# One low-part operation per dense value block, written over its raw block, with four raw buffers and products of 512, 512 and 384 columns

## The chip, the cores and the metric

The kernel runs on one core of a Trainium2 chip. A core has five engines with an instruction stream each: TensorE (PE; its weight loads are listed apart as PEld), VectorE (DVE), ScalarE (ACT), GpSimd (POOL) and SyncE (SP), which here issues the plain DMAs. They meet only at semaphores. Sixteen DMA engines move data between the chip's memory (HBM) and the on-chip buffer of 128 partitions (SBUF). Products are accumulated in PSUM. The metric is the time of one execution on the device in microseconds (us); lower is better.

## The reference

One layer of a hybrid encoder over 256 tokens of width 2048: an RMS norm, one combined projection, forgetting attention and a gated recurrence, their merge with an output projection, and then a PEER layer, a second residual and a final RMS norm. The change touches the last part of the PEER layer alone:

```python
def peer_layer(x, wq, keys, U, Vt):
    ...
    # for each token: 8 heads x 16 experts, idx (T, 8, 16) out of 16384, gate = softmax of their scores
    def blk(args):
        xb, ib, gb = args
        u = U[ib]
        hid = jax.nn.gelu(jnp.einsum('td,thkd->thk', xb, u))
        v = Vt[ib]
        return jnp.einsum('thk,thkd->td', gb * hid, v)
```

Each token thus adds 128 rows of the value table `Vt` (16384 x 2048), each with its own weight `gb * hid`.

## The kernel before

All work is float32. Where TensorE multiplies, an operand is split into a high part, its rounding to the type `fp32r`, and a low part, the rest; a product is the sum of high x high, high x low and low x high.

The value sum is done in two ways at once. Of each row of `Vt` the last 640 columns (`CW`) are fetched only for the experts that were chosen: GpSimd issues 256 indirect DMAs (2 token tiles x 128 choices), each of 128 rows of 640 columns, 328 KB, into a ring of five buffers `starts`, and VectorE multiplies each with its token's weight and adds it to `X` (line 1411; `add_start(s)`). The first 1408 columns (`DW`) are done densely. The 16384 experts are 128 blocks of 128. For each block the whole 128 x 1408 piece of the table (721 KB) is loaded, and multiplied from the left with a 128 x 256 matrix of weights (expert of the block by token, most entries zero), which an earlier stage has scattered into `weight_of`.

For block `n` the engines do this, each in the order of its own loop over the blocks:

- SP loads `v_raw[n % 3]` (line 363). From block 3 on it first waits on `v_ready` until both low parts of block n - 3 are written.
- ScalarE writes the high part `v_hi[n % 2]` (line 771) when the load has landed and block n - 2 is used up. Before every even block it also writes `e_hi`, the high parts of the weights of two blocks (line 762).
- VectorE writes the low part in two pieces, 768 and 640 columns, into a single buffer `v_lo` (line 1420). Each piece waits for `v_used`, until TensorE has used the same piece of the block before. Behind each piece stands one `add_start`. After every second block come two operations for `e_lo` (line 1400).
- TensorE (lines 1770 to 1772) does for each piece and each of the two token tiles (`acc` for the first, `scr` for the second, both in PSUM) three products for each run of columns: 512 and 256 in the first piece, 256 and 384 in the second. It adds one to `v_used` after each piece. That is 24 products a block.

GpSimd issues the gather for `starts[s % 5]` (line 487) when `x_added` says that add s - 5 is done. So the gather for s + 5 starts after add s. An add waits for its gather and for the add before it.

The code is written out in this order, with no scheduler; each engine goes through its own list.

## Time and profile before

| | us |
|---|---|
| three runs | 2193.09, 2183.55, 2193.47; median 2193.09 |
| profiled execution | 2183.11, span 2181.4 |
| PE busy | 1477.1 (68%) |
| DVE busy | 1641.9 (75%) |
| ACT busy | 837.4 (38%) |
| POOL busy | 975.7 (45%) |
| dense loads, 128 of 704 KB, from issue to landing | 6.4 (median) |
| gathers of 640 columns, 256, from issue to landing | 6.6 (median) |

The profile is that of one execution. Its busy shares are means over stages that have different limits: projections up to some 870 us, the gathers and dot products for the hidden values up to about 1600 us, and from 1663 to 2164 us the stage that the change touches. An engine's instruction is followed in the views by what ended the idle time before it. Starts and durations overlap somewhat on VectorE and TensorE, because an instruction begins before the one ahead of it has written all its results; so the distance from start to start is what one costs in a row.

### The profile page before, as it was taken

Reading aid. Unit: us, or ns where it says so; the run is one execution under the profiler, and the core shown is the slowest. Engines: PE = TensorE matmul, PEld = TensorE weight load, DVE = VectorE, ACT = ScalarE, POOL = GpSimd, SP = SyncE. Lnnn points to the kernel's source line nnn. Section 1 sums busy time; section 2 is a strip of 40 time slices with the busy share of each in tenths; the row PEclk is TensorE's granted clock in tenths of the full one; section 3 lists DMA queues with packets and bytes.
Section 4 is the critical chain, followed back from the end, with each engine's and each line's share of the span. In section 5 each row is a group of like instructions: output and inputs, shape, how many; then the busy total and the mean of one; then the engine's idle time right before and its main releaser. Section 6 shows DMA issues by size and latency. Waiting matters only on the chain.

```text
span 2181.4 us, 26401 instructions
## 1 busy us (share of the span) xinstructions
PE 1477.1 (68%) x9809; PEld 1368.3 (63%) x9809; DVE 1641.9 (75%) x2172; ACT 837.4 (38%) x1008; POOL 975.7 (45%) x692
## 2 busy tenths in 40 slices
PE   6999999999999999700000000113358999999996
PEld 6987998899999889700000000113247999899996
DVE  5465774545654555798898899998878999999997
ACT  4353433333433444112121221446666444444443
POOL 1002220000000000188888878877747776667763
PEclk9999999999999999855555555555569999999998
DMA  5555443434455554399999999999905999999996
GB/s 194 173 175 191 137 153 126 155 136 158 171 174 175 194 192 168 144 422 421 418 415 414 416 386 404 419 404 369 359 26 191 357 359 354 346 369 356 360 357 224
DMA packets 151526, 597.80 MB, mean 274 GB/s; under 512 B 14688, under 2 KB 14704, under 8 KB 118000
## 3 DMA queue, kind: packets, MB, share of 16 engines
q0 software_dynamic: 58048, 356.02, 41.3%
q1 hardware_dynamic: 93360, 240.22, 31.2%
q8 instruction: 72, 1.18, 0.2%
q14 instruction: 46, 0.38, 0.0%
HBM read 594.09 MB, written 2.10 MB: 273 GB/s over the span
## 4 chain that ended last, share of the span: by engine, by line
PE 47%; issue 15%; DVE 14%; DMA 11%; POOL 8%; ACT 4%; DVEq 0%; POOLq 0%; SPq 0%; ACTq 0%
PE acc L1470 9%; PE acc L1473 8%; PE acc L1472 8%; DMA slots<-in_peer_u,expert 8%; DVE slots L1331 7%; POOL starts L487 6%; DMA starts<-in_v_gather,expert 3%; PE acc L1487 3%; PE acc L1489 3%; PE acc L1488 3%; PE scr L1740 3%; POOL slots L450 1%; PE scr L1535 1%; PE acc L1770 1%; PE acc L1772 1%
## 5 line engine op out<-in xcount | busy, mean ns | idle before, releaser
L798 DVE TENSOR_TENSOR w_lo<-raw,w_hi 128x2048 fp32r<-128x2048 f32 x136 | 314.7, 2315 | 319.5 <-ACT w_hi L503 318.5
L1331 DVE SCALAR_TENSOR_TENSOR slots<-slots,acc 128x2048 f32<-128x2048 f32 x189 | 428.3, 2284 | 36.4 <-DMA slots<-in_peer_u,expert 34.6
L503 ACT ACTIVATE w_hi<-raw 128x2048 fp32r<-128x2048 f32 x136 | 260.1, 1913 | 435.6 <-PE acc L1473 308.0
L487 POOL DMA_INDIRECT starts<-in_v_gather,expert x256 | 344.5, 1346 | 155.4 <-DVE X L1411 103.8
L450 POOL DMA_INDIRECT slots<-in_peer_u,expert x256 | 250.5, 979 | 288.8 <-DVE expert L1267 188.4
L458 POOL TENSOR_TENSOR slots<-slots,N 128x2048 f32<-128x2048 f32 x63 | 285.6, 4533 | 31.6 <-DMA slots<-in_peer_u,expert 31.2
L1470 PE MATMUL acc<-hT_hi,w_hi 128*128 128x256 f32 x1024 | 294.6, 288 | 3.1 <-PE acc L1473 2.5
L1472 PE MATMUL acc<-hT_lo,w_hi 128*128 128x256 f32 x1024 | 292.2, 285 | 0.0
L1473 PE MATMUL acc<-hT_hi,w_lo 128*128 128x256 f32 x1024 | 292.1, 285 | 0.0
L1740 PE MATMUL scr<-hot_a,hot_b 128*128 128x128 f32 x512 | 101.4, 364 | 280.5 <-ACT hot_a L732 171.9
L771 ACT ACTIVATE v_hi<-v_raw 128x1408 fp32r<-128x1408 f32 x128 | 177.0, 1384 | 282.3 <-PE scr L1772 203.6
L1740 PEld LDWEIGHTS scr<-hot_a,hot_b 128*128 128x128 f32 x512 | 88.8, 263 | 293.3 <-issue 283.1
L698 ACT ACTIVATE slots<-slots 128x2048 f32<-128x2048 f32 x63 | 120.3, 1910 | 393.1 <-POOL slots L458 393.1
L1420 DVE TENSOR_TENSOR v_lo<-v_raw,v_hi 128x768 fp32r<-128x768 f32 (+1 forms) x256 | 227.6, 889 | 31.6 <-PE scr L1772 27.9
L1411 DVE SCALAR_TENSOR_TENSOR X<-starts,weight,X 128x640 f32<-128x640 f32 x256 | 225.1, 879 | 8.5 <-DMA starts<-in_v_gather,expert 8.3
L1470 PEld LDWEIGHTS acc<-hT_hi,w_hi 128*128 128x128 f32 x1024 | 199.1, 194 | 5.7 <-issue 5.7
L1472 PEld LDWEIGHTS acc<-hT_lo,w_hi 128*128 128x128 f32 x1024 | 199.0, 194 | 0.0
L1473 PEld LDWEIGHTS acc<-hT_hi,w_lo 128*128 128x128 f32 x1024 | 198.8, 194 | 0.0
L1770 PE MATMUL acc<-v_hi,e_hi 128*128 128x256 f32 (+2 forms) x512 | 167.7, 328 | 8.2 <-DVE v_lo L1420 8.1
L1772 PE MATMUL acc<-v_hi,e_lo 128*128 128x256 f32 (+2 forms) x512 | 165.9, 324 | 0.0
L1771 PE MATMUL acc<-v_lo,e_hi 128*128 128x256 f32 (+2 forms) x512 | 165.7, 324 | 0.0
L1771 PE MATMUL scr<-v_lo,e_hi 128*128 128x256 f32 (+2 forms) x512 | 165.6, 323 | 0.0
(262 smaller groups left out, 3324.1 us busy)
## 6 DMA issues: line engine op xcount, KB each, us to landing
raw<-in_w_in SPq DMA_DIRECT2D x88, 1024.0 KB, 4.8
v_raw<-in_v_dense SPq DMA_DIRECT2D x128, 704.0 KB, 6.4
raw<-in_w_o SPq DMA_DIRECT2D x16, 1024.0 KB, 5.1
raw<-in_peer_wq SPq DMA_DIRECT2D x16, 1024.0 KB, 5.0
raw<-in_w_a_up SPq DMA_DIRECT2D x8, 1024.0 KB, 5.1
raw<-in_w_b_up SPq DMA_DIRECT2D x8, 1024.0 KB, 5.0
slots<-in_peer_u,expert POOLq DMA_INDIRECT x256, 9.0
starts<-in_v_gather,expert POOLq DMA_INDIRECT x256, 6.6
```

The lines of the kernel that those rows point to most:

```text
L450: pool.indirect_dma_start(slots[:, j, :], None, u_rows, bass.IndirectOffsetOnAxis(ap=expert[:, t, k:k + 1], axis=0)).then_inc(row_landed[j ...
L458: g.tensor_tensor(slots[:, j, :], slots[:, j, :], N1[:, q // NSEL, :], ALU.mult).then_inc(product_ready, 1)
L487: pool.indirect_dma_start(starts[s % CRING][:, :], None, v_gather[:, :], bass.IndirectOffsetOnAxis(ap=expert[:, s // NSEL, s % NSEL:s % NS ...
L503: a.activation(w_hi[:, m % 2, :, :], raw[:, m % 2, :, :], ACT.Copy).then_inc(hi_ready, 1)
L798: v.tensor_tensor(w_lo[:, m % 2, :, :], raw[:, m % 2, :, :], w_hi[:, m % 2, :, :].bitcast(fp32), ALU.subtract).then_inc(lo_ready, 1)
L1331: v.scalar_tensor_tensor(out=slots[:, j, :], in0=slots[:, j, :], scalar=1.0, in1=row, op0=ALU.mult, op1=ALU.mult, accum_out=hid[:, t, k:k + 1]
L1420: v.tensor_tensor(v_lo[:, cols], v_raw[n % RAWS][:, cols], v_hi[:, n % 2, cols].bitcast(fp32), ALU.subtract).then_inc(v_ready, 1)
L1470: t_.matmul(to, wh, hi_[:, kk, :], start=kk == 0 and f % 2 == 0, stop=False, skip_group_check=True)
L1472: t_.matmul(to, wh, lo_[:, kk, :], start=False, stop=False, skip_group_check=True)
L1473: last = t_.matmul(to, wl, hi_[:, kk, :], start=False, stop=last_k, skip_group_check=True)
L1740: last = t_.matmul(scr[:, n % 2, (SC + c) * P:(SC + c + 1) * P], hot_b[:, n % 2, c, :], hot_a1[:, n % 4, c, :] if t else hot_a[:, n % 2, c ...
L1771: t_.matmul(to, eh, v_lo[:, cols], start=False, stop=False, skip_group_check=True)
```

## The change

The low part of a block is written by one VectorE operation of 1408 columns instead of two. It goes into the same memory as the block's raw data: `v_lo[n]` is a view at the address of `v_raw[n]`, of which there are now four (the fourth lies where the single `v_lo` was). The operation no longer waits for `v_used`. Both `add_start` of a block stand behind it, one after the other. TensorE waits for `v_ready` once a block, does its three products for runs of 512, 512 and 384 columns for each token tile, and adds one to `v_used` at the block's end. Since the raw buffer now also holds the low part, SP waits for `v_used` of block n - 4 before it loads block n. ScalarE's and GpSimd's waits on `v_used` are restated in blocks.

```diff
--- before.py
+++ after.py
@@ -49,12 +49,11 @@
 SC = 4
 CW = 640
 DW = D - CW
-VHALF = (slice(0, 768), slice(768, DW))
-VPIECES = (((0, 512), (512, 768)), ((768, 1024), (1024, DW)))
+VPIECES = ((0, 512), (512, 1024), (1024, DW))
 BLOCKS = P
 BATCHES = P // SC
 CRING = 5
-RAWS = 3
+RAWS = 4
 PIECES = 4
 SPREAD_FROM, SPREAD_TWICE = 44, 52
 IJ_GROUP = 56
@@ -206,8 +205,10 @@
         weight_of1 = at("weight_of1", 32, [P, P])
         weight_of = [[at(f"weight_of0_{q}", kib, [P // PIECES, P]) for q, kib in enumerate((16, 128, 144, 168))],
                      [weight_of1[:, q * P // PIECES:(q + 1) * P // PIECES, :] for q in range(PIECES)]]
-        v_raw = [at(f"v_raw{n}", kib, [DW]) for n, kib in enumerate((112, 117.5, 105))]
-        v_hi, v_lo = at("v_hi", 184, [2, DW], f32r), at("v_lo", 160, [DW], f32r)
+        VALUES_AT = (112, 117.5, 105, 160)
+        v_raw = [at(f"v_raw{n}", kib, [DW]) for n, kib in enumerate(VALUES_AT)]
+        v_lo = [at(f"v_lo{n}", kib, [DW], f32r) for n, kib in enumerate(VALUES_AT)]
+        v_hi = at("v_hi", 184, [2, DW], f32r)
         e_hi, e_lo = at("e_hi", 97, [2, NT, 2 * P], f32r), at("e_lo", 101, [2, NT, 2 * P], f32r)
         gain_f = at("gain_f", 16, [D])
         starts = [at(f"starts{n}", kib, [CW]) for n, kib in enumerate((123, 125.5, 195, 197.5, 165.5))]
@@ -368,8 +369,9 @@
             load_v(1)
             sp.wait_ge(scattered, 2 + NT * P // SC)
             load_v(2)
+            load_v(3)
             for n in range(RAWS, BLOCKS):
-                sp.wait_ge(v_ready, 2 * (n - RAWS) + 2)
+                sp.wait_ge(v_used, n - RAWS + 1)
                 sp.sem_inc(granted_w, 1)
                 load_v(n)
             for n in range(2 * NT):
@@ -476,7 +478,7 @@
 
             for s in range(NT * NSEL):
                 if s == NSEL:
-                    pool.wait_ge(v_used, 2 * P // PIECES)
+                    pool.wait_ge(v_used, P // PIECES)
                     pool.dma_start(gain_f[:, :], norm_f_g.rearrange("(l f) -> l f", l=1).partition_broadcast(P)
                                    .rearrange("q l f -> q (l f)")).then_inc(gain_f_in, 16)
                 if s == CRING - 1:
@@ -756,7 +758,7 @@
             def high_e(pair):
 
                 if pair >= 2:
-                    act.wait_ge(v_used, 4 * pair - 4)
+                    act.wait_ge(v_used, 2 * pair - 2)
                 q, at0 = 2 * pair // (P // PIECES), 2 * pair % (P // PIECES)
                 for t in range(NT):
                     last = a.activation(e_hi[:, pair % 2, t, :],
@@ -767,7 +769,7 @@
             for n in range(BLOCKS):
                 act.wait_ge(v_landed[n % RAWS], 16 * (n // RAWS + 1))
                 if n >= 2:
-                    act.wait_ge(v_used, 2 * (n - 2) + 2)
+                    act.wait_ge(v_used, n - 1)
                 a.activation(v_hi[:, n % 2, :], v_raw[n % RAWS][:, :], ACT.Copy).then_inc(v_hi_ready, 1)
                 if n % 2 and n + 1 < BLOCKS:
                     high_e((n + 1) // 2)
@@ -1414,18 +1416,17 @@
             low_e(0)
             for n in range(BLOCKS):
                 dve.wait_ge(v_hi_ready, n + 1)
-                for c, cols in enumerate(VHALF):
-                    if n:
-                        dve.wait_ge(v_used, 2 * (n - 1) + c + 1)
-                    v.tensor_tensor(v_lo[:, cols], v_raw[n % RAWS][:, cols], v_hi[:, n % 2, cols].bitcast(fp32),
-                                    ALU.subtract).then_inc(v_ready, 1)
-                    add_start(2 * n + c)
+                lows = v_lo[n % RAWS][:, :]
+                v.tensor_tensor(lows, v_raw[n % RAWS][:, :], v_hi[:, n % 2, :].bitcast(fp32),
+                                ALU.subtract).then_inc(v_ready, 1)
+                add_start(2 * n)
+                add_start(2 * n + 1)
                 if n % 2 and n + 1 < BLOCKS:
                     low_e((n + 1) // 2)
             dve.wait_ge(x_added, NT * NSEL)
 
             y = [acc[:, :, :].rearrange("p a n -> p (a n)"), scr[:, :, :].rearrange("p a n -> p (a n)")]
-            dve.wait_ge(v_used, 2 * BLOCKS)
+            dve.wait_ge(v_used, BLOCKS)
             for t in range(NT):
                 v.tensor_tensor(X[:, t, CW:D], y[t][:, 0:DW], X[:, t, CW:D], ALU.add).then_inc(y_summed, 1)
             dve.wait_ge(squared, 1 + 4 * NT + NT)
@@ -1759,19 +1760,17 @@
             for n in range(BLOCKS):
                 pe.wait_ge(e_ready, n // 2 + 1)
                 e_cols = slice(n % 2 * P, (n % 2 + 1) * P)
-                for c in range(2):
-                    pe.wait_ge(v_ready, 2 * n + c + 1)
-                    for t in range(NT):
-                        flat = (acc, scr)[t][:, :, :].rearrange("p a n -> p (a n)")
-                        eh, el = e_hi[:, n // 2 % 2, t, e_cols], e_lo[:, n // 2 % 2, t, e_cols]
-                        for at0, end in VPIECES[c]:
-                            to, cols = flat[:, at0:end], slice(at0, end)
-                            clear, stop = n == 0 and at0 % GW == 0, n == BLOCKS - 1
-                            t_.matmul(to, eh, v_hi[:, n % 2, cols], start=clear, stop=False, skip_group_check=True)
-                            t_.matmul(to, eh, v_lo[:, cols], start=False, stop=False, skip_group_check=True)
-                            last = t_.matmul(to, el, v_hi[:, n % 2, cols], start=False, stop=stop,
-                                             skip_group_check=True)
-                    last.then_inc(v_used, 1)
+                pe.wait_ge(v_ready, n + 1)
+                for t in range(NT):
+                    flat = (acc, scr)[t][:, :, :].rearrange("p a n -> p (a n)")
+                    eh, el = e_hi[:, n // 2 % 2, t, e_cols], e_lo[:, n // 2 % 2, t, e_cols]
+                    for at0, end in VPIECES:
+                        to, cols = flat[:, at0:end], slice(at0, end)
+                        clear, stop = n == 0, n == BLOCKS - 1
+                        t_.matmul(to, eh, v_hi[:, n % 2, cols], start=clear, stop=False, skip_group_check=True)
+                        t_.matmul(to, eh, v_lo[n % RAWS][:, cols], start=False, stop=False, skip_group_check=True)
+                        last = t_.matmul(to, el, v_hi[:, n % 2, cols], start=False, stop=stop, skip_group_check=True)
+                last.then_inc(v_used, 1)
 
 
 _INS = ["x", "norm1_g", "w_in", "fox_f_bias", "hg_lb_logits", "hg_norm_g", "w_a_up", "w_b_up", "w_o", "norm2_g",
```

VectorE's rows in the dense stage, before, for an odd block and the even one behind it; each row is an operation with what it writes and reads, the columns, and the semaphores it waits for:

```order
L1420 TENSOR_TENSOR v_lo_81<-v_raw2_79,v_hi_80 128x768 [waits v_used,v_hi_ready]
L1411 SCALAR_TENSOR_TENSOR X_49<-starts0_85,weight_91,X_49 128x640 [waits x_added,start_landed0]
L1420 TENSOR_TENSOR v_lo_81<-v_raw2_79,v_hi_80 128x640 [waits v_used]
L1411 SCALAR_TENSOR_TENSOR X_49<-starts1_86,weight_91,X_49 128x640 [waits x_added,start_landed1]
L1400 TENSOR_TENSOR e_lo_83<-weight_of0_0_73,e_hi_82 128x256 [waits e_hi_ready]
L1400 TENSOR_TENSOR e_lo_83<-weight_of1_72,e_hi_82 128x256
L1420 TENSOR_TENSOR v_lo_81<-v_raw0_77,v_hi_80 128x768 [waits v_used,v_hi_ready]
```

and now, for such a block and the one behind it:

```order
L1420 TENSOR_TENSOR v_lo3_84<-v_raw3_80,v_hi_85 128x1408 [waits v_hi_ready]
L1413 SCALAR_TENSOR_TENSOR X_49<-starts4_93,weight_95,X_49 128x640 [waits x_added,start_landed4]
L1413 SCALAR_TENSOR_TENSOR X_49<-starts0_89,weight_95,X_49 128x640 [waits x_added,start_landed0]
L1402 TENSOR_TENSOR e_lo_87<-weight_of0_0_73,e_hi_86 128x256 [waits e_hi_ready]
L1402 TENSOR_TENSOR e_lo_87<-weight_of1_72,e_hi_86 128x256
L1420 TENSOR_TENSOR v_lo0_81<-v_raw0_77,v_hi_85 128x1408 [waits v_hi_ready]
```

The second add has lost the operation that stood between it and the first, and the low part its wait for `v_used`.

TensorE's rows for the second token tile (`scr`) in a block's first piece, before, and the row that begins the second piece with a wait of its own (3 x 256 and 3 x 384 columns for `acc` and then for `scr` make up that piece):

```order
L1770 MATMUL scr<-v_hi_80,e_hi_82 128x512
L1771 MATMUL scr<-v_lo_81,e_hi_82 128x512
L1772 MATMUL scr<-v_hi_80,e_lo_83 128x512
L1770 MATMUL scr<-v_hi_80,e_hi_82 128x256
L1771 MATMUL scr<-v_lo_81,e_hi_82 128x256
L1772 MATMUL scr<-v_hi_80,e_lo_83 128x256
L1770 MATMUL acc<-v_hi_80,e_hi_82 128x256 [waits v_ready]
```

and now, the same tile with the start of the next block behind it:

```order
L1770 MATMUL scr<-v_hi_85,e_hi_86 128x512
L1771 MATMUL scr<-v_lo1_82,e_hi_86 128x512
L1772 MATMUL scr<-v_hi_85,e_lo_87 128x512
L1770 MATMUL scr<-v_hi_85,e_hi_86 128x512
L1771 MATMUL scr<-v_lo1_82,e_hi_86 128x512
L1772 MATMUL scr<-v_hi_85,e_lo_87 128x512
L1770 MATMUL scr<-v_hi_85,e_hi_86 128x384
L1771 MATMUL scr<-v_lo1_82,e_hi_86 128x384
L1772 MATMUL scr<-v_hi_85,e_lo_87 128x384
L1770 MATMUL acc<-v_hi_85,e_hi_86 128x512 [waits v_ready,e_ready]
```

A tile's nine products stand together now, and the wait in the middle of a block is gone.

## Rows read from the trace of the kernel before

**Rows 1.** The page's 40 slices of 54.5 us: PE's busy tenths, and transfers.
```profile
PE   6999999999999999700000000113358999999996
...
GB/s 194 173 175 191 137 153 126 155 136 158 171 174 175 194 192 168 144 422 421 418 415 414 416 386 404 419 404 369 359 26 191 357 359 354 346 369 356 360 357 224
```

**Rows 2.** Windows: length; PE, PEld, DVE, ACT, POOL busy; PEclk; DMA share; GB/s.
```profile
1900.00:1950.00 50.00, 49.10 (x305) 45.37 (x304) 45.23 (x63) 20.99 (x27) 35.12 (x27) 1.00 0.98 375
1950.00:2000.00 50.00, 50.00 (x313) 46.48 (x312) 46.81 (x67) 21.63 (x25) 35.82 (x27) 1.00 0.97 356
```

**Rows 3.** Timeline of TensorE, dense stage: start, duration, engine, line, operation.
```profile
1984.77 0.40 PE L1770 MATMUL acc<-v_hi,e_hi 128*128 128x512 f32 x1
...
1985.47 0.28 PE L1770 MATMUL acc<-v_hi,e_hi 128*128 128x256 f32 x1
...
1985.82 0.39 PE L1770 MATMUL scr<-v_hi,e_hi 128*128 128x512 f32 x1
...
1986.86 0.28 PE L1770 MATMUL acc<-v_hi,e_hi 128*128 128x256 f32 x1
...
1987.22 0.34 PE L1770 MATMUL acc<-v_hi,e_hi 128*128 128x384 f32 x1
...
1988.63 0.40 PE L1770 MATMUL acc<-v_hi,e_hi 128*128 128x512 f32 x1
```

**Rows 4.** Timeline of TensorE in a projection: first and last of 53 products.
```profile
788.21 0.39 PE L1487 MATMUL acc<-w_hi,hT_hi 128*128 128x512 f32 x1
...
800.00 0.39 PE L1488 MATMUL acc<-w_lo,hT_hi 128*128 128x512 f32 x1
```

**Rows 5.** Timeline of VectorE in the dense stage.
```profile
1987.13 0.96 DVE L1420 TENSOR_TENSOR v_lo<-v_raw,v_hi 128x768 fp32r<-128x768 f32 x1 [0.54 <-PE scr L1772]
1988.01 0.88 DVE L1411 SCALAR_TENSOR_TENSOR X<-starts,weight,X 128x640 f32<-128x640 f32 x1
1988.83 0.83 DVE L1420 TENSOR_TENSOR v_lo<-v_raw,v_hi 128x640 fp32r<-128x640 f32 x1
...
1995.80 0.88 DVE L1411 SCALAR_TENSOR_TENSOR X<-starts,weight,X 128x640 f32<-128x640 f32 x1
...
1997.35 0.88 DVE L1411 SCALAR_TENSOR_TENSOR X<-starts,weight,X 128x640 f32<-128x640 f32 x1
1998.15 0.75 DVE L1400 TENSOR_TENSOR e_lo<-weight_of,e_hi 128x256 fp32r<-128x256 f32 x2
1998.82 0.95 DVE L1420 TENSOR_TENSOR v_lo<-v_raw,v_hi 128x768 fp32r<-128x768 f32 x1
```

**Rows 6.** Timeline of ScalarE in the dense stage.
```profile
1988.89 1.38 ACT L771 ACTIVATE v_hi<-v_raw 128x1408 fp32r<-128x1408 f32 x1 [1.87 <-PE scr L1772]
```

**Rows 7.** Timeline of VectorE at the end: the final sums, then small chained operations.
```profile
2164.67 1.62 DVE L1430 TENSOR_TENSOR X<-acc,X 128x1408 f32<-128x1408 f32 x1 [2.31 <-PE scr L1772]
2166.21 1.61 DVE L1430 TENSOR_TENSOR X<-scr,X 128x1408 f32<-128x1408 f32 x1
...
2172.38 0.16 DVE L812 TENSOR_TENSOR stat<-stat 128x2 f32<-128x2 f32 x1
2172.57 0.16 DVE L813 TENSOR_TENSOR stat<-stat 128x2 f32<-128x2 f32 x1
```

**Rows 8.** Waits from 1660 to 2170 us: total us, times, longest.
```profile
ACT v_hi L771 <- DMA v_raw<-in_v_dense: 78.7, 34, 3.4
...
DVE X L1411 <- DMA starts<-in_v_gather,expert: 8.3, 7, 2.8
```

**Rows 9.** Timeline of GpSimd: two issues of gathers.
```profile
1989.70 1.57 POOL L487 DMA_INDIRECT starts<-in_v_gather,expert  x1 [0.79 <-DVE X L1411]
...
2127.63 1.18 POOL L487 DMA_INDIRECT starts<-in_v_gather,expert  x1 [3.44 <-issue]
```

**Rows 10.** Line 487, landings: the gather issued at 1989.70; all from 1700 to 2150.
```profile
DMA to landing us min/median/max: 7.3/7.3/7.3
...
DMA to landing us min/median/max: 5.0/6.7/10.0
```

## The prediction, made before the changed kernel ran

> **What bounds the kernel now.** I read the page's slices first, to find which stretch the change touches and what is busy there: from the slice at 1690 us on TensorE stands at nine tenths, at 350 GB/s of transfers [rows 1] and with its full clock [rows 2]. That stretch is the dense value stage, 128 blocks from 1663 to 2164 us. The rest of the program keeps its instructions. Then I read TensorE's timeline, because an engine at 100% need not be the bound: a block's first product starts at 1984.77 and the next block's at 1988.63 [rows 3], so a block takes 3.86 us, and in a quiet window TensorE is busy 50.00 of 50 us [rows 2]. 128 x 3.86 = 494 us; the stage lasts 501. TensorE sets the pace, and 7 us are lost in a first block at half clock and a few stalls.
>
> Who stands close behind? Per block VectorE has two `v_lo` subtractions and two adds of a gathered row part to X (I call them the even and the odd add, by their number s), and after every second block two `e_lo` of together 0.67 us (1998.15 to 1998.82) [rows 5]. An add followed by another instruction costs 0.80 us from start to start (1997.35 to 1998.15), the even add together with the 640-column subtraction behind it 1.55 (1995.80 to 1997.35). The DMA engines are at 0.97 of their time with 356 GB/s [rows 2]; a block brings 0.721 MB dense and two gathers of 0.328 MB, 1.376 MB in 3.86 us.
>
> **Products (the term that should gain).** Per block 24 matmuls become 18, over the same 6 x 1408 columns. What goes is, for each of the two token tiles, six products of 256 columns, and three of 512 come. Rows 3: three 256-column products take 0.35 us (1985.47 to 1985.82) or 0.36 (1986.86 to 1987.22), so six take 0.71; three of 512 take 0.70 (1984.77 to 1985.47). That alone saves 0.01 us a tile. The products of 512 right behind an equal one are somewhat quicker than those after a change of tile: in the projection stage 52 of them take 11.79 us, 0.227 each [rows 4], three 0.68. I take 0.694 for three, between the two and nearer to this stage's rows: 0.016 a tile, 0.03 a block, a period of 3.83 and 128 x 0.03 = -4 us. Bounds: -0 us, if a merged product costs what two halves do; with all twelve at 0.227 the saving is 2 x (0.71 - 0.68) = 0.06, and 0.08 with the four that are there today sped up too, -10 us.
> The Trainium skill ("TensorE: Matmul & The Clock Gate", section "Wait — 56ns, not 53.3ns?") gives a warm product a fixed 2.5 ns beside its columns. By it six fewer would be worth 15 ns a block, 1.9 us in all; the row in the projection stage shows about 14 ns above 512 columns at 2.4 GHz, so trace and page differ, and the sum above uses neither.
>
> **VectorE.** Subtractions of 768 and 640 columns become one of 1408. The trace has no SBUF subtraction of that length; the final sums of 1408 columns take 1.62 us, and the second starts 1.54 after the first [rows 7]. So one costs 1.54 where two cost 0.88 (1987.13 to 1988.01) and 1.55 - 0.80 = 0.75, 1.63 together. But now the odd add directly follows the even one and waits for it by `x_added`. Small chained instructions show what such a wait costs: 0.16 us long, 0.19 apart (2172.38 and 2172.57) [rows 7], so the even add holds the odd one for 0.88 + 0.03 = 0.91 instead of 0.80. Per block 1.54 + 0.91 + 0.80 = 3.25, plus 0.67 every second time: 7.17 us in two blocks against 7.66 of TensorE. What fusing saves, the adds' wait takes back; VectorE stays hidden, value nothing. The wait of the subtraction for `v_used`, 0.54 us at 1987.13, goes, since each block has a low part of its own. What is late in its place is the high part: ScalarE's starts 0.26 us after the next block's products (1988.63, 1988.89) and lasts 1.38 [rows 6], the subtraction then 1.62 and 0.15 of signals to TensorE, 3.41 of 3.83. Reserve 0.4 us, if VectorE is free in time. After a block with `e_lo` it frees 3.92 after its own subtraction, 0.1 later than that, so its reserve is 0.3; after the others 0.9.
>
> **Start.** TensorE's first product waits for the whole low part, 1.62 instead of the 0.96 of its first piece (1987.13) [rows 5]: +0.7 us.
>
> **Raw buffers.** A load was issued after the second subtraction, with three buffers; now it is issued when TensorE has finished the block four back, with four. The second subtraction of a block starts at 1988.83 and lasts 0.83 us [rows 5]; it ends 1.0 us after that block's products began at 1988.63. Now the end of the block before, at that same 1988.63, releases the load: it leaves 1 us earlier relative to its use. SP has nothing else queued. ScalarE waited for such loads 34 times, 78.7 us in all [rows 8], nearly all of it in its own idle time; this gets shorter. Value: -1 us of the stalls, bounds -3 and 0.
>
> **Gathers (the term that should cost).** Five row buffers; the gather for s + 5 leaves when add s is done. Even add 1988.01, 0.88 long; the gather starts at 1989.70 after 0.79 of idle time [rows 9], lands 7.3 us later at 1997.0 [rows 10], and its odd add starts at 1997.35. Now that odd add would start 0.91 behind its even one at 1995.80, at 1996.71: this gather is 0.3 us late. With the line's median of 6.7 [rows 10] it is 0.3 early. A gather for an even add keeps the distance that it had. So the change uses up the margin of every second gather, and VectorE's reserve (0.3 or 0.9 us) catches the lateness. A landing above about 7.3 us then costs TensorE time in the blocks with `e_lo`, above 7.9 in the others; landings go to 10.0. I estimate that a quarter of the 64 narrow blocks lose 0.2 us, 3 us, and that the stalls that exist (seven late adds, 8.3 us, one behind a 3.44 us pause of GpSimd before it issues [rows 8, 9]) cost 2 us more since 0.6 us less is there to absorb them. Together +5, bounds 0 and +20 (rival below).
>
> **Sum.** -4 + 0.7 - 1 + 5 = +0.7. The profiled execution took 2183.1 us (span 2181.4), so about 2184 on its level. The three runs have one at that level (2183.55) and two at 2193, whose median is 10 us above. I don't know which level the changed kernel's runs fall on and take 2188.
>
> **Rivals.**
> 1. The products gain in full and the gathers keep up. For it: 0.227 us each for 52 products in a row, and VectorE's idle time in this stage. Against it: in this stage 512 columns take 0.233. Then -10 + 0.7 - 2 = -11 us, with the same levels 2172 to 2182.
> 2. Slower: the ring of gathers becomes the bound. The loop is even add, gather, odd add, the next subtraction, even add, over three blocks: 0.88 + 0.81 + landing + 0.03 + 0.80 + half of 0.67 + 1.54 = landing + 4.40. It decides from a landing of 3 x 3.83 - 4.40 = 7.09 us. Before, 0.88 for the 768 columns stood in it instead of 1.54: landing + 3.74, so it would have taken 3 x 3.86 - 3.74 = 7.84 us. With 7.5 us on average it gives 3.97 us a block, 128 x 0.14 = +18, about 2201 (2197 to 2207). For it: 7.3 in rows 10, and loads that are asked for earlier. Against it: the median 6.7, and that a later request meets a shorter queue.
> 3. The DMA engines are the bound and nothing moves. At 3.83 us they must bring 359 GB/s with a share near 0.98. Against it: 375 GB/s at 0.98 just before [rows 2], and 414 to 424 in the stage of long rows [rows 1]. It would give 3.86 us a block, 2184 plus the stalls, 2189 in the runs.
> The Trainium skill ("DMA: Bandwidth & Descriptors", section "Where 436 GB/s comes from") puts a core's share of HBM at about 358 GB/s. By that rule a block could not go below 3.84 us, which is rival 3; the trace's 375 and 424 disagree with it as a limit for one core alone.
>
> **How the numbers follow.** Forecast 0.48, rival 1 0.24, rival 2 0.18, rival 3 0.10. A measurement of this kernel can tell about 0.5%, 11 us, from no change. Rival 1 lies at that border and the two levels of the runs add to either side: faster 0.26, same 0.54, slower 0.20. The likeliest case spans 2180 to 2196. The range reaches to rival 1 on one side and most of rival 2 on the other: 2171 to 2203.
>
> **What would show it.** Right: products of 512 at 0.23 us, a block at 3.83, odd adds 0.91 behind even ones, no wait of the subtraction for `v_used`, fewer waits of ScalarE for dense loads, more waits of adds for gathers (8.3 us becoming 20 or more). Wrong: a block at 3.78 (rival 1); TensorE's windows below 48 us with the subtraction's wait passed on from late adds (rival 2); a block at 3.86 with full DMA (rival 3). The forecast fails as a whole if late adds are absent, or if every third block shows TensorE idle.

## The result, and the profile after

Over 14 runs each, the changed kernel takes 2200.65 us (2197.94 to 2207.62) and the kernel before 2190.8 (2183.55 to 2195.42): a ratio of 1.0054, 95% interval 1.0043 to 1.0066. Another 12 runs of it gave 2198.8 and 1.0035 (1.0019 to 1.0052). It is slower by some 10 us; I had forecast no change, likeliest between 2180 and 2196 us, with 2203 as the upper end of the range. Its profiled execution took 2198.78 us.

The slices of the page, as in [rows 1]:

```profile
PE   6999999999999999600000000113358999999996
...
GB/s 193 172 175 189 142 147 133 146 154 149 165 168 187 195 176 169 175 422 421 418 414 417 400 361 404 417 402 363 349 14 212 354 347 350 349 355 350 353 353 226
```

In the stage's slices the transfers have gone from 346 to 369 GB/s to 347 to 355; PE's tenths don't resolve more than one place. The windows that answer to [rows 2], same columns:

```profile
1900.00:1950.00 50.00, 47.17 (x218) 39.44 (x217) 43.54 (x50) 20.27 (x24) 32.37 (x26) 1.00 0.96 358
1950.00:2000.00 50.00, 49.27 (x231) 42.19 (x230) 45.50 (x51) 21.32 (x25) 34.82 (x25) 1.00 0.97 350
```

TensorE, which had filled 49.10 and 50.00 of 50 us, is idle for 2.8 and 0.7 us of them, at the same full clock. The products themselves are quicker. TensorE's timeline, the first of each group of three, as in [rows 3]:

```profile
1974.70 0.40 PE L1770 MATMUL acc<-v_hi,e_hi 128*128 128x512 f32 x1
1975.39 0.40 PE L1770 MATMUL acc<-v_hi,e_hi 128*128 128x512 f32 x1
...
1976.62 0.40 PE L1770 MATMUL scr<-v_hi,e_hi 128*128 128x512 f32 x1
...
1978.54 0.40 PE L1770 MATMUL acc<-v_hi,e_hi 128*128 128x512 f32 x1
```

A block takes 3.84 us (1974.70 to 1978.54) against 3.86. The stage nevertheless lasts 508.3 us from its first product to the end of its last, against 501.5; in the second profile of the changed kernel 512.0. 128 blocks at 3.84 are 491.5, so 16.8 and 20.5 us are lost, where before it was 501.5 - 494.1 = 7.4. In each of the three profiles some 1.4 to 1.6 us of the loss is the first block, which takes 5.3 to 5.5 us. The waits of the stage, as in [rows 8]:

```profile
ACT v_hi L773 <- DMA v_raw<-in_v_dense: 38.1, 16, 3.8
DVE X L1413 <- DMA starts<-in_v_gather,expert: 28.9, 36, 2.5
PE acc L1770 <- DVE v_lo L1420: 13.4, 14, 4.9
DVE v_lo L1420 <- ACT v_hi L773: 9.9, 28, 1.3
```

The adds' waits for gathers have gone from 8.3 us to 28.9 (30.9 in the second profile). ScalarE's for dense loads are 38.1 and 70.4 in the two profiles, 78.7 before: they say nothing by themselves, since they lie in ScalarE's idle time unless they pass it.

The profile of the changed kernel starts the dense stage 8.5 us later than that of before. 0.7 of this is the longer first low part. The rest lies where the program is the same, and the second profile has only 3.3: that part is scatter between executions, and the page of before comes from one of its quickest. The second profile was taken to decide this. I had expected 2200.7 us in all, a stage that begins between 1663 and 1671 us if it is scatter, and a stage of 506 to 510 us; measured were 2198.8, 1666.4 and 512.0, so the start is as expected, while the stage came out 2 us longer than the span that I gave.

How one late add becomes a stall can be read from VectorE's and GpSimd's timelines:

```profile
1977.92 1.86 DVE L1413 SCALAR_TENSOR_TENSOR X<-starts,weight,X 128x640 f32<-128x640 f32 x2
1979.60 1.00 POOL L489 DMA_INDIRECT starts<-in_v_gather,expert  x1 [0.79 <-DVE X L1413]
1979.70 0.75 DVE L1402 TENSOR_TENSOR e_lo<-weight_of,e_hi 128x256 fp32r<-128x256 f32 x2
1980.37 1.61 DVE L1420 TENSOR_TENSOR v_lo<-v_raw,v_hi 128x1408 fp32r<-128x1408 f32 x1
1980.91 1.90 POOL L489 DMA_INDIRECT starts<-in_v_gather,expert  x1 [0.30 <-issue]
1981.91 1.87 DVE L1413 SCALAR_TENSOR_TENSOR X<-starts,weight,X 128x640 f32<-128x640 f32 x2
...
1984.06 1.63 DVE L1420 TENSOR_TENSOR v_lo<-v_raw,v_hi 128x1408 fp32r<-128x1408 f32 x1 [0.28 <-ACT v_hi L773]
1984.90 1.61 POOL L489 DMA_INDIRECT starts<-in_v_gather,expert  x1 [0.30 <-issue]
1985.60 0.88 DVE L1413 SCALAR_TENSOR_TENSOR X<-starts,weight,X 128x640 f32<-128x640 f32 x1
...
1987.72 0.89 DVE L1413 SCALAR_TENSOR_TENSOR X<-starts,weight,X 128x640 f32<-128x640 f32 x1 [1.24 <-DMA starts<-in_v_gather,expert]
1988.52 0.75 DVE L1402 TENSOR_TENSOR e_lo<-weight_of,e_hi 128x256 fp32r<-128x256 f32 x2
1989.19 1.62 DVE L1420 TENSOR_TENSOR v_lo<-v_raw,v_hi 128x1408 fp32r<-128x1408 f32 x1
```

The gather issued at 1979.60 lands after 8.1 us, and its odd add begins at 1987.72 after 1.24 us of waiting. `e_lo` and the low part follow, ready at 1990.81, and TensorE, which had begun the block before at 1986.22 and could have gone on at 1990.06, does so in the row below: 4.73 us for a block.

```profile
1990.95 0.48 PE L1770 MATMUL acc<-v_hi,e_hi 128*128 128x512 f32 x1 [0.73 <-DVE v_lo L1420]
```

The same rows show what I had overlooked. GpSimd's issues (L489) do not all last equally long: 1.00 at 1979.60, 1.90 at 1980.91, 1.61 at 1984.90. The ends follow a rule. 1980.91 + 1.90 = 1982.81 is 0.83 behind the end of the low part that was running (1980.37 + 1.61 = 1981.98); 1984.90 + 1.61 = 1986.51 is 0.82 behind 1985.69; 1979.60 + 1.00 is 0.82 behind the end of the pair of adds, 1979.78. Of the 227 issues that begin between 1700 and 2150 us, 211 begin while a VectorE instruction runs, and 208 of these end 0.78 to 0.86 us behind the end of that instruction (218 of 223 in the profile before: in [rows 9], 1989.70 + 1.57 = 1991.27, the add begun at 1989.57 ends at 1990.45). The 16 that begin beside none take 0.94 or 0.95 us. So in this stage an issue that begins beside a VectorE instruction is held until that one ends. The longest thing to be held by is now 1.62 us, and was 0.96.

### The profile page after: what moved, and what is told of

Same layout as the page of the kernel before. It is cut to its first block, busy times and chain, and to the rows that moved or that the text cites. A ratio compares the mean times of both kernels' runs of the same rounds, so it can differ in the third digit from the quotient of the medians.

```text
span 2196.7 us, 24609 instructions
## 1 busy us (share of the span) xinstructions
PE 1480.2 (67%) x9041; PEld 1331.4 (61%) x9041; DVE 1643.1 (75%) x2044; ACT 837.5 (38%) x1008; POOL 978.2 (45%) x692
## 4 chain that ended last, share of the span: by engine, by line
PE 42%; issue 16%; DVE 15%; DMA 14%; POOL 9%; ACT 4%; POOLq 0%; DVEq 0%; SPq 0%; ACTq 0%
PE acc L1471 9%; PE acc L1474 8%; PE acc L1473 8%; DMA slots<-in_peer_u,expert 8%; POOL starts L489 7%; DVE slots L1333 7%; DMA starts<-in_v_gather,expert 6%; PE acc L1488 3%; PE acc L1490 3%; PE acc L1489 3%; PE scr L1741 3%; POOL slots L452 2%; PE scr L1536 1%; DVE X L1413 1%; ACT weight_of L722 1%
## 5 line engine op out<-in xcount | busy, mean ns | idle before, releaser
L489 POOL DMA_INDIRECT starts<-in_v_gather,expert x256 | 345.0, 1348 | 161.9 <-DVE X L1413 124.3
L1413 DVE SCALAR_TENSOR_TENSOR X<-starts,weight,X 128x640 f32<-128x640 f32 x256 | 225.6, 881 | 39.8 <-DMA starts<-in_v_gather,expert 28.9
L1420 DVE TENSOR_TENSOR v_lo<-v_raw,v_hi 128x1408 fp32r<-128x1408 f32 x128 | 207.4, 1620 | 10.2 <-ACT v_hi L773 9.9
L1770 PE MATMUL acc<-v_hi,e_hi 128*128 128x512 f32 (+1 forms) x384 | 147.8, 385 | 13.8 <-DVE v_lo L1420 13.4
L1770 PE MATMUL scr<-v_hi,e_hi 128*128 128x512 f32 (+1 forms) x384 | 145.0, 378 | 0.0
L1772 PE MATMUL acc<-v_hi,e_lo 128*128 128x512 f32 (+1 forms) x384 | 144.6, 377 | 0.0
L1772 PE MATMUL scr<-v_hi,e_lo 128*128 128x512 f32 (+1 forms) x384 | 144.3, 376 | 0.0
```

Of the source, the lines that this page charges most:

```text
L489: pool.indirect_dma_start(starts[s % CRING][:, :], None, v_gather[:, :], bass.IndirectOffsetOnAxis(ap=expert[:, s // NSEL, s % NSEL:s % NS ...
L1770: t_.matmul(to, eh, v_hi[:, n % 2, cols], start=clear, stop=False, skip_group_check=True)
L1772: last = t_.matmul(to, el, v_hi[:, n % 2, cols], start=False, stop=stop, skip_group_check=True)
```

## The experiments

All were run against the kernel before, whose medians lay at 2189.8 to 2191.2 us; three kernels were run twice. The stage's length is that of one profile each, from the first product to the end of the last.

**More room for gathers.** First edit, against the changed kernel (the main lines; one more finds the free place, and the wait for `scattered` stays ahead of the fifth gather):

```diff
-CRING = 5
+CRING = 6
+        starts.append(nc.alloc_sbuf_tensor_at("starts5", [P, CW], fp32, offset=spare_at))
```

> The changed kernel with six row buffers for the gathers instead of five (the sixth lies over constants that are dead by then). Theory G (the odd add now follows the even one at 0.91 us, so the gather for it has 0.6 us less to land, and the lateness reaches TensorE): waits of adds for gathers fall from 28.9 us to under 5, the dense stage from 508 to 494 to 497 us, the ratio to the kernel before from 1.0054 to 0.998 to 1.001. Theory D (the dense loads, which leave 1 us earlier, push ahead of the gathers): a partial gain, gather landings as long as in the changed kernel or longer, ratio 1.001 to 1.004. Theory F (the fused low part of 1.62 us is itself too late for TensorE): no gain, ratio 1.004 to 1.006. Theory U (the 7.9 us that the changed kernel was behind ahead of the first dense product are lasting, not scatter): not below 1.002.

Measured 2187.75 us, ratio 0.9989 (0.9974 to 1.0005), stage 503.0:

```profile
DVE X L1415 <- DMA starts<-in_v_gather,expert: 5.1, 6, 2.5
```

12 us are back and most of the late adds are gone: the ratio is as theory G had it. The stage of this profile is not, 503.0 where 494 to 497 was expected; its execution took 2192.2, one of the slower of twelve, and ScalarE waited 85.0 us for dense loads. Theories D, F and U all had 1.001 or more and fall as they were put. The ring of gathers is where the change loses.

**Loads held back.** In the changed kernel SP asks for a dense load one high part later:

```diff
+                sp.wait_ge(v_hi_ready, n - 1)
                 sp.wait_ge(v_used, n - RAWS + 1)
```

> The changed kernel, with one wait more ahead of each dense load: SP also waits for v_hi of block n - 2, which puts the load some 1.4 us later, near where it was before. Theory G: nothing is won, waits of adds for gathers stay above 22 us, stage 506 to 510 us, ratio to before 1.004 to 1.007. Theory D: gathers for even adds land in 6.5 us or less again (7.6 in the changed kernel, 6.1 before), waits for gathers under 15 us, ratio 1.001 or less. Theory F: as the changed kernel.

Measured 2225.08, ratio 1.0164 (1.0140 to 1.0187), stage 537.6:

```profile
ACT v_hi L774 <- DMA v_raw<-in_v_dense: 271.0, 106, 4.1
...
DVE X L1414 <- DMA starts<-in_v_gather,expert: 8.9, 17, 1.3
```

The dense loads come far too late: what they lead by is needed. The adds' waits do fall below 15 us, as theory D had it and theory G did not, but TensorE now stands for some 30 us more, which gives every gather more time. So the run does not decide whether the earlier loads also delay gathers.

**The parts of the change one by one.** e3 has the four buffers, the low part in place and the merged products, but two low parts with an add behind each, and TensorE begins on the first (TensorE's loop over the two pieces, as in the kernel before, is left out here):

```diff
-VPIECES = ((0, 512), (512, 1024), (1024, DW))
+VPIECES = (((0, 512),), ((512, 1024), (1024, DW)))
-                v.tensor_tensor(lows, v_raw[n % RAWS][:, :], ...).then_inc(v_ready, 1)
-                add_start(2 * n)
-                add_start(2 * n + 1)
+                for c, cols in enumerate(VHALF):
+                    v.tensor_tensor(v_lo[n % RAWS][:, cols], ...).then_inc(v_ready, 1)
+                    add_start(2 * n + c)
```

> The changed kernel's four raw buffers, low parts in place and products of 512, 512 and 384 columns, but the low part in two operations of 768 and 640 columns as before, each with one add behind it; TensorE does the first 512 columns of both token tiles when the first is there and the rest when the second is. Theory G: adds are 1.55 us apart again, waits for gathers back at 10 us or less, stage 497 to 500 us, ratio 0.997 to 1.000. Theory D: as the changed kernel, ratio 1.003 or more, since the loads still leave early. Theory F: as by G.

> The kernel of e3_two_lows once more (one add behind each low part), for a second profile and twice the runs. Theory G (adjacent adds make every second gather late): total below that of e4's kernel by 2 to 8 us and a stage of 499 to 503 us with 15 to 20 us of late adds. Rival (where the adds stand is without effect, and the 7.7 us between the stages of e3 and e4 were scatter): the two agree within 1.5 us in total and in their second stages.

Measured 2190.64, 0.9999 (0.9981 to 1.0017), stage 499.0; again 2189.13, 0.9987 (0.9974 to 1.0001), stage 504.0. The late adds of the two profiles:

```profile
DVE X L1414 <- DMA starts<-in_v_gather,expert: 16.6, 28, 2.1
```
```profile
DVE X L1414 <- DMA starts<-in_v_gather,expert: 22.9, 36, 2.8
```

The total is that of the kernel before, as expected, but the late adds are not: 10 us or less was expected, and with the adds where they always stood they rise from 8.3 us to 16.6 and 22.9. So a part of the rise does not come from where the adds stand.

e4 moves both adds behind the two low parts:

```diff
-                    add_start(2 * n + c)
+                add_start(2 * n)
+                add_start(2 * n + 1)
```

> The same kernel as e3_two_lows with both adds behind the two low-part operations, next to each other, as in the changed kernel. Theory G: as the changed kernel, waits of adds for gathers 22 us or more, stage 505 to 510 us, ratio 1.003 to 1.006, and clearly slower than e3_two_lows. Theory D: no difference from e3_two_lows, both slow. Theory F: no difference from e3_two_lows, both at 1.000 or below, since the first piece is ready early in either.

> The kernel of e4_two_lows_adjacent once more, for a second profile and twice the runs. Theory G: stage 504 to 508 us with 22 to 30 us of late adds, total 2192 to 2196. Rival: stage 499 to 503 us, total as c3_two_lows_again.

Measured 2192.23, 1.0003 (0.9989 to 1.0017), stage 506.7; again 2192.94, 1.0012 (0.9998 to 1.0026), stage 504.3, late adds 24.7 and 22.9 us. Waits and stages are near theory G, the total is not: 1.003 or more and clearly slower than e3 was expected, and e4 is 1.6 and 3.8 us slower in the two pairs, of which only the second is clear of the noise. e10 then lets TensorE begin a block only when both are written:

```diff
-                    pe.wait_ge(v_ready, 2 * n + c + 1)
+                    pe.wait_ge(v_ready, 2 * n + 2)
```

> The kernel of e4_two_lows_adjacent (two low parts of 768 and 640 columns in place, both adds behind them), in which TensorE starts a block only when both low parts are written, as the changed kernel does with its one low part. It asks what the changed kernel has more than e4: 2200 against 2192. Theory F (the first piece of a block no longer comes early, so the same late adds meet less reserve): 2198 to 2201, ratio 1.0035 to 1.0055. Rival (the two operations of 768 and 640 take less of VectorE or of its partners than the one of 1408, and where TensorE waits is without effect): ratio 1.000 to 1.0015, 2190 to 2193.

Measured 2193.32, 1.0012 (0.9999 to 1.0025), stage 502.2. My theory F falls: I had expected 2198 to 2201. With e10 everything of the change is in place but two things, that the low part is one operation and that TensorE does all nine products of a token tile together. e11 settles which. It is the changed kernel with:

```diff
-                v.tensor_tensor(lows, v_raw[n % RAWS][:, :], ...).then_inc(v_ready, 1)
+                for at0, end in ((0, 768), (768, DW)):
+                    low = v.tensor_tensor(v_lo[n % RAWS][:, at0:end], ...)
+                low.then_inc(v_ready, 1)
```

> The changed kernel with the low part of a block in two VectorE operations of 768 and 640 columns, one right behind the other; TensorE's products, waits, buffers and the adds stay as changed. Theory H (an issue of a gather ends 0.82 us behind the end of the VectorE instruction that ran when it began, so the operation of 1408 columns, 1.62 us, holds every second issue): these issues fall from 1.65 us to about 1.3, their gathers land 0.4 to 0.6 us sooner, the stage becomes 501 to 506 us and the total that of e10, 2191 to 2195, ratio 1.000 to 1.002. Rival J (the order of TensorE's products, all nine of a token tile together, makes the difference to e10): 2198 to 2201, although the issues get shorter.

Measured 2192.95, 1.0013 (1.0000 to 1.0026), stage 504.6. One cut in one VectorE instruction is worth 7 us (9.0 against the first set of runs of the changed kernel, 4.8 against the second). Rival J falls. GpSimd's issues from 1700 to 2150 us (idle before them behind the second bar) and the adds' waits, first of the changed kernel (its waits are above), then of e11:

```profile
L489 POOL DMA_INDIRECT starts<-in_v_gather,expert x228 | 310.2, 1360 | 140.8 <-DVE X L1413 108.2 <-issue 32.6
```
```profile
L489 POOL DMA_INDIRECT starts<-in_v_gather,expert x230 | 268.1, 1166 | 181.8 <-DVE X L1413 128.0 <-issue 53.8
...
DVE X L1413 <- DMA starts<-in_v_gather,expert: 12.3, 18, 2.3
```

An issue takes 0.19 us less on the mean; the even gathers' go from 1.63 to 1.30, the odd ones' from 1.08 to 1.03. This profile does not tell when e11's gathers landed, so that they land 0.4 to 0.6 us sooner is not shown for e11 itself. In e11's timeline the issue begins beside the same low part and ends behind its first half (1962.97 + 1.23 = 1964.20; the 768 columns take 0.96 from 1962.42 and end at 1963.38):

```profile
1962.42 1.69 DVE L1420 TENSOR_TENSOR v_lo<-v_raw,v_hi 128x768 fp32r<-128x768 f32 x2
1962.97 1.23 POOL L489 DMA_INDIRECT starts<-in_v_gather,expert  x1 [0.30 <-issue]
```

e12 cuts it in four of 352 columns:

> The changed kernel with the low part in four VectorE operations of 352 columns. Theory H: every operation lasts about 0.47 us, so an issue beside them is held for less still, near 1.0 to 1.1 us instead of 1.65; VectorE pays some 0.05 us for each cut. Total 2188 to 2194, not above e11. Rival (what counts is VectorE's own length, 3.25 us a block, and each cut makes it longer): above e11 by 2 us or more, with fewer and longer waits of TensorE for the low part. Rival J: 2198 or more, as e11.

Measured 2194.59, 1.0020 (1.0007 to 1.0033), stage 509.1. The issues shrink again, as theory H has it, and late adds to 7.5 us. But the median block takes 3.905 us. TensorE's start at 1963.81 releases the high part, and the low part follows it at once, lasts 1.83 and ends at 1967.30. With 0.15 of signals TensorE could go on at 1967.45, and it is free at 1967.71: a reserve of 0.26.

```profile
1963.81 0.47 PE L1771 MATMUL acc<-v_hi,e_hi 128*128 128x512 f32 x1
1964.06 1.38 ACT L773 ACTIVATE v_hi<-v_raw 128x1408 fp32r<-128x1408 f32 x1 [2.45 <-PE scr L1773]
...
1965.47 1.83 DVE L1420 TENSOR_TENSOR v_lo<-v_raw,v_hi 128x352 fp32r<-128x352 f32 x4
...
1967.71 0.40 PE L1771 MATMUL acc<-v_hi,e_hi 128*128 128x512 f32 x1
```
```profile
L489 POOL DMA_INDIRECT starts<-in_v_gather,expert x227 | 243.7, 1073 | 205.9 <-DVE X L1413 138.3 <-issue 67.6
```

The chain of high part, low part and product, 3.41 us by the forecast, is 3.64 here, and in every other block or so nothing is left of its reserve: 64 of 125 blocks start within 0.2 us of the end of their low part (the one at 1963.81 is 0.15 behind it), where in e11 24 do and in the changed kernel 34. The first product of such a block then takes 0.07 us longer (0.47 instead of 0.40). So both the theory and the rival had a share. The total lies between what the two had forecast, 1.6 us above e11, which is within the noise: one piece is worse than two, and four are not shown to be better or worse than two.

**Other prices.** e9 takes the semaphore increment (line 488) out of GpSimd's loop:

> The changed kernel without the semaphore increment that GpSimd makes between its wait for an add and the issue of the next gather. In the profile the issue starts 0.79 us after the add's end. Theory G: if part of the 0.79 us is this instruction, every gather leaves earlier and the late adds (28.9 us) fall, by about 8 us for each 0.1 us gained at first; with 0.1 us gained total 2194 to 2198. Rival: the increment costs nothing and the 0.79 us is the way of the semaphore and the issue itself; then 2200, and 28 us of waits.

Measured 2195.89, 1.0023 (1.0007 to 1.0039), stage 502.9, late adds 18.2 us: the total is in the range expected, 2.9 us below the changed kernel's runs of the same set, which by itself is within the noise, and 4.3 below all its runs. But an issue now lasts 1.52 on the mean instead of 1.36, since it starts sooner beside the same VectorE instruction: the hold eats part of the lead.

e7 shortens the gathers themselves (the changed kernel; from the sixth on):

```diff
-                pool.indirect_dma_start(starts[s % CRING][:, :], None, v_gather[:, :],
+                wide = CW if s < CRING else CW // 4
+                rows = v_gather[:, :] if s < CRING else v_gather.rearrange("n (q c) -> (n q) c", q=4)
+                pool.indirect_dma_start(starts[s % CRING][:, 0:wide], None, rows,
```

> The changed kernel with gathers of a quarter: from the sixth on each brings rows of 160 columns (82 KB, from another place of the table) where 640 were fetched; the adds still go over 640 columns, on what the buffer holds. The result is therefore another. All engines' instructions, the ring of five and the order stay; the DMA engines lose 0.246 MB of each gather, 0.49 MB of a block's 1.376. Theory G+F (the loss is late gathers and nothing in the engines' own order): no late adds and no waits for dense loads, period 3.83 to 3.84, stage 128 x 3.84 + 2 to 5 = 493 to 497, total 2183 to 2187. Rival (VectorE's own chain, 3.25 us a block with both adds adjacent and e_lo, or ScalarE's high part, costs TensorE time even with data in place): stage 500 or more, total above 2190.

Measured 2182.81, 0.9971 (0.9955 to 0.9986), stage 492.0:

```profile
1950.00:2000.00 50.00, 50.00 (x237) 43.11 (x236) 46.88 (x52) 22.50 (x28) 42.05 (x27) 1.00 0.72 230
```
```profile
DVE X L1415 <- DMA starts<-in_v_gather,expert: 0.7, 2, 0.4
```

With transfers at 230 GB/s TensorE never stops and a block takes 3.827 us in 9 of 10 cases. The engines' order has nothing against it: the rival, 2190 or more, falls, and both numbers lie at or just below the lower end of what theory G+F gave. The issues are held as ever, 1.54 on the mean: the hold costs only where the gathers have no slack.

**Six buffers with the rest.** The kernel before with six:

> The kernel before with a sixth gather buffer and nothing else. Theory G: the kernel before had only 8.3 us of late adds, so there is little to win: the stage falls by at most 3 us, total ratio 0.998 to 1.001, and the waits of the adds go from 8.3 us to under 4. Rival (the ring of gathers was a common limit of both kernels and the sixth buffer is worth the same 13 us here): ratio 0.994, stage near 490.

Measured 2187.13, 0.9979 (0.9965 to 0.9992), stage 499.7, no late adds: as theory G had it, the gain of 3 us at its edge. e11 with six:

> e11 with six gather buffers: the changed kernel, low part in two operations. Theory H: with six buffers no gather is late by the hold, so what it gains on e1_ring6 (2187.8) is small, 0 to 3 us: 2184 to 2188, ratio 0.997 to 0.999. Rival (a cut low part is worth its 7 us with six buffers too): 2181 or less. It is also the candidate for the best version beside e5_two_lows_ring6 (2182.9), which lets TensorE begin on the first piece.

Measured 2184.00, 0.9970 (0.9956 to 0.9984), stage 498.0: against e1 the median is 3.7 us lower, where 0 to 3 was expected; twelve runs each do not tell this from nothing. And e3 with six:

> The kernel with two low parts of 768 and 640 columns in place and one add behind each, now with six gather buffers. Theory G+F (late gathers, and a low part of 1.62 us as one piece that leaves little reserve against them): both causes are gone, the block period is TensorE's 3.84 us, the stage from its first product to its last end about 128 x 3.84 + 6 = 498 us, like e3_two_lows (499.0), the adds' waits for gathers fall from 16.6 us to under 6. Total 2186 to 2190, ratio to the kernel before 0.998 to 1.000. If G alone held, it would be equal to e1_ring6 (2187.8) too. Rival D (the DMA engines are the bound, and what the ring gives to the gathers it takes from the dense loads): ScalarE's waits for dense loads rise from 15.1 us towards 85 as in e1_ring6 and the stage gets no shorter than 499, or longer.

Measured 2182.93, 0.9963 (0.9947 to 0.9979), stage 494.5, better than forecast by 3 us. Its windows and all its waits of the stage on transfers:

```profile
1900.00:1950.00 50.00, 49.94 (x234) 42.54 (x232) 46.41 (x66) 21.66 (x25) 35.52 (x27) 1.00 0.99 379
1950.00:2000.00 50.00, 50.00 (x235) 43.06 (x234) 46.20 (x65) 22.27 (x27) 35.82 (x27) 1.00 0.97 359
```
```profile
ACT v_hi L776 <- DMA v_raw<-in_v_dense: 9.0, 4, 3.1
```

No add waits. It beats both kernels, by 7 us the one before and by 17 the changed one, and is some 4 us below the kernel before with six buffers (2187.1), which the whole change with six (2187.8) does not beat.

## Why the prediction was wrong

In medians, with all runs of a kernel pooled, the way from the kernel before to the changed one is: 2190.5, in-place low parts, four buffers and merged products (e3) 2189.7, adds together (e4) 2192.4, TensorE waiting for the whole low part (e10) 2193.3, products tile by tile (e11) 2193.0, one low part 2200.2. A step is known to some 2.5 us, so of these only the last, +7.2 (4.9 to 9.1), is beyond doubt; the adds' +2.7 is at the border.

- **Products, -4.** Right in mechanism. A block of 3.827 us in e7 is the 3.83 forecast; in the changed kernel, beside full transfers, it is 3.84, which makes -2.6.
- **Start, +0.7.** Right: from the start of the first low part to the first product it was 1.11 us and is 1.77.
- **VectorE, nothing.** Right for VectorE itself: the low part lasts 1.62; the wait for `v_used` is gone, and the reserve of TensorE is the 0.4 forecast (low part ready at 1985.69, 0.15 of signals, start at 1986.22, which leaves 0.38). The odd add begins 0.98 behind the even one (median), not 0.91: a pair lasts 1.86 to 1.87, so a wait on the operation just ahead costs 0.10, where I had 0.03 from very short ones. That is 0.07 a block of VectorE's idle time. What I asked was too little: "What fusing saves, the adds' wait takes back" counts VectorE's own time, and the instruction's length also acts on GpSimd.
- **Raw buffers, -1.** Not seen as a gain, and not tested by itself. In the stage the changed kernel's dense loads land after 7.3 us (median), before after 6.4; e2 shows that their lead cannot be spared. e3, with the same early loads and quicker products, is no faster than the kernel before and has more late adds, which suggests that something in it costs about what the products gain; whether it is the early loads stays open.
- **Gathers, +5: the step that failed.** The place was right. The late ones are every second gather, as forecast: of 42 adds that began within 0.03 us of the landing of their gather 38 are odd (44 of 45 in the second profile). The waits rose to 28.9 us, as said under "20 or more". The size was not: what the stage loses rose by 16.8 - 7.4 = 9.4 us in one profile and by 13.1 in the other, where +5 - 1 = +4 was forecast. (The start's 0.7 us lies ahead of the first product, outside the stage.) With the products' -2.6 and the start's +0.7 that makes +7.5 and +11.2; the runs have +9.7. Both halves of the +5 were too small. "A quarter of the 64 narrow blocks lose 0.2 us": 19 of the blocks behind an `e_lo` took over 3.94 us in one profile and 23 in the other, a little over a quarter, but they lost 0.31 and 0.44 us each, and what these blocks lose rose by 5.3 and 8.9 us instead of 3. The other blocks lost 4.2 and 4.1 us more instead of 2.

What I had not asked is whether the change alters the landings themselves. I had taken 6.7 us from the trace before. It is 7.2 now ([rows 10] is its counterpart):

```profile
DMA to landing us min/median/max: 4.7/7.2/10.5
```
and in e10, with the low part in two pieces, 6.6:
```profile
DMA to landing us min/median/max: 4.2/6.6/9.3
```

By parity this reads otherwise than the two medians suggest. Even gathers landed after 6.1 us before, after 7.6 in the changed kernel and 7.0 in e10; odd ones, which are the late ones, after 6.95 before, 6.8 in the changed kernel and 6.3 in e10 (7.3 and 6.5 in the second profile of e4, which has the same adds). So against the kernel before the odd gathers do not land later; their add comes sooner, 0.98 us behind the even one instead of 1.55, as forecast. Against the same order with the low part in two pieces, however, they land 0.3 to 0.5 us later, and the margin of the median odd gather shrinks from 0.77 us in e10 to 0.27. That is what the long operation takes away, and what the forecast lacked.

The landing counts from the start of the issue, and of the 0.6 us that even gathers land later than in e10 the held issue is about half (1.63 instead of 1.31 on the mean). The odd one's issue is short in both, 1.08 and 1.02; that it lands later as well suggests that it queues behind the delayed one. The runs do not show that step by itself. What they show is its two ends: the length of one VectorE operation sets how long the issue beside it lasts, and cutting that operation gives 7 us back.

The Trainium skill ("SBUF — State Buffer", section "Who interferes with whom") says that a VectorE instruction with two SBUF inputs contends with a GpSimd instruction that reads SBUF, and its section "Summary: rules for kernel authors" that the second of the two to issue is blocked until the first finishes. The low part has two SBUF inputs and the indirect DMA takes its row numbers from SBUF; the traces agree where the GpSimd instruction comes second, with 0.82 us between the end of the one and the end of the other. The section "Who interferes with whom" also infers that such a subtraction does not hold up the writing of descriptors. Here the issue of an indirect DMA is held, with a median of 1.74 us beside 1408 columns against 1.24 beside the two pieces of e11; whether it is its reading or its writing that waits, no run here separates.

- **The rivals.** Rival 2 had the sign and, with 2201 (2197 to 2207), the time. Its mechanism was half right: the ring of gathers is the place, but not as a bound on every block, since the median block stays at 3.84 and one in ten takes over 4.16 us; and in the loop that it names (the odd gathers) the landing is 6.8, below the 7.09 from which it would decide. Rival 1 is refuted in both its parts in the changed kernel. Rival 3 is refuted: e5 moves 379 GB/s in a window, and e7 with free transfers is only 0.02 us a block quicker than e5. (The 424 GB/s held against it are not in [rows 1], whose highest is 422; nothing hangs on the difference.)
- **The level of the runs.** All runs of the kernel before have the median 2190.5, 7 us above the profiled execution. I had put 4 us on top of it for this, 2188 on 2184, so 3 us of the 12.7 between forecast and measurement are the level and not the change.

## What to carry to other kernels

Before two operations of an engine are merged, look at what another engine does beside them: here one VectorE instruction of 1.62 us held the issue of GpSimd's next gather until it had ended, and a cut that costs VectorE 0.07 us gave 7 us back. Where a ring of transfers has a margin of a few tenths of a microsecond, do not take the landing time of the trace as given; ask what the change does to the issue. Give the ring one more buffer first: with six the kernel before takes 2187.1 us, the whole change 2187.8, and the change with two low parts and an add behind each 2182.9.

## What the runs showed of the hardware

In the dense stage of these kernels an indirect DMA's issue on GpSimd takes 0.94 or 0.95 us when it begins beside no VectorE instruction, and otherwise ends 0.82 us behind the end of the one beside which it began (208 of 211): in the median 1.23 us beside a low part of 768 columns, 1.74 and up to 2.33 beside one of 1408. All VectorE instructions of this stage read two operands from SBUF, so that the runs do not tell what others do. The hold is there whether or not the transfers are loaded (e7), and also in the kernel before, where its odd gathers' issues took 1.48 us without my asking why.
